# Output projection, feed-forward and down projection with features on partitions, the second norm applied when PSUM is emptied, and four waits moved

## What is computed

```
h = rms_norm(x, g_mix);  z = h @ w_in             # q, k, v (3 groups), u, two gates
a_out = dilated_attention(q, k, v) @ w_attn_proj
y = gelu(s5_ssm(u));  s_out = (y @ w_glu_a) * sigmoid(y @ w_glu_b)
mix = sigmoid(gate_a) * a_out + sigmoid(gate_s) * s_out
x = x + mix @ w_out                               # "x1" in the kernel
h2 = rms_norm(x, g_ffn)
x = x + (silu(h2 @ w_ffn_gate) * (h2 @ w_ffn_up)) @ w_ffn_down     # D_FF = 2816
```

## Time and profile before

| | |
|---|---|
| median of three runs | 916.68 us |
| the profiled execution | 918.38 us, its span 916.5 us |
| PE busy | 885.2 us, 97% of the span |
| DVE, ACT, POOL busy | 423.3, 349.1, 178.6 us |
| mean share of the 16 DMA engines busy | under 40% |
| mean granted clock of TensorE | 0.993 |

### The profile page before, as it was taken

How to read it: one execution, slowest core, us unless ns; L and a number is a source line. 1 busy time by engine, 2 the same in 40 slices (tenths; PEclk the granted TensorE clock), 3 DMA queues, 4 the chain that set the end, 5 groups by cost and what they waited for, 6 DMA issues and landing times.

```text
span 916.5 us, 12956 instructions
## 1 busy us (share of the span) xinstructions
PE 885.2 (97%) x4488; PEld 726.2 (79%) x4488; DVE 423.3 (46%) x583; ACT 349.1 (38%) x514; POOL 178.6 (19%) x223
## 2 busy tenths in 40 slices
PE   5988999999999999998999989999999999999998
PEld 4876888888797877876887867888888888888886
DVE  6575566677804444543468344322223222333333
ACT  5311343323325656754533235333333333322221
POOL 4699978710020000001220020000000000000000
PEclk9999999999999999998999999999999999999999
DMA  7338344574454552411224323223322233222222
GB/s 274 106 94 209 117 136 137 150 189 137 143 147 145 168 154 77 133 69 51 106 77 160 115 69 92 92 92 98 108 92 92 92 104 102 92 92 92 92 69 92
DMA packets 84511, 106.64 MB, mean 116 GB/s; under 512 B 10464, under 2 KB 51600, under 8 KB 84480
## 3 DMA queue, kind: packets, MB, share of 16 engines
q1 hardware_dynamic: 79904, 96.34, 33.6%
q10 hardware_dynamic: 3168, 6.29, 2.1%
q0 software_dynamic: 1408, 3.61, 1.9%
HBM read 92.29 MB, written 13.93 MB: 116 GB/s over the span
## 4 chain that ended last, share of the span: by engine, by line
PE 49%; DVE 2%; DMA 1%; ACT 1%; issue 1%; POOL 0%; SPq 0%; POOLq 0%; DVEq 0%; ACTq 0%
PE ps L1407 26%; PE ps L1421 13%; PE ps L1148 10%; DMA late<-in_x 1%; DVE late L1130 1%; DVE w_lo L550 1%; ACT hT_hi L583 0%; PE ps L1373 0%; ACT w_hi L544 0%; DVE late L1073 0%; DVE hT_lo L1079 0%; PE ps L1310 0%; POOL row_ss L415 0%; POOL row_r L416 0%; PE ps L1296 0%
## 5 line engine op out<-in xcount | busy, mean ns | idle before, releaser
L550 DVE TENSOR_TENSOR w_lo<-w_raw,w_hi 128x1024 fp32r<-128x1024 f32 x142 | 199.8, 1408 | 382.1 <-ACT w_hi L544 380.4
L544 ACT ACTIVATE w_hi<-w_raw 128x1024 fp32r<-128x1024 f32 x142 | 150.3, 1059 | 415.4 <-PE ps L1148 174.7
L1148 PE MATMUL ps<-w_hi,hT_hi 128*128 128x512 f32 x352 | 139.1, 395 | 17.2 <-DVE w_lo L550 17.2
L1407 PE MATMUL ps<-hT_hi,w_hi 128*128 128x512 f32 x352 | 137.1, 390 | 2.0 <-DVE hT_lo L787 1.6
L1148 PE MATMUL ps<-w_lo,hT_hi 128*128 128x512 f32 x352 | 138.0, 392 | 0.0
L1148 PE MATMUL ps<-w_hi,hT_lo 128*128 128x512 f32 x352 | 138.0, 392 | 0.0
L1407 PE MATMUL ps<-hT_hi,w_lo 128*128 128x512 f32 x352 | 137.0, 389 | 0.0
L1407 PE MATMUL ps<-hT_lo,w_hi 128*128 128x512 f32 x352 | 136.9, 389 | 0.0
L400 POOL TENSOR_TENSOR early<-early 128x16 f32<-128x16 f32 (+8 forms) x141 | 124.2, 881 | 23.1 <-ACT early L567 12.1
L1148 PEld LDWEIGHTS ps<-w_hi,hT_hi 128*128 128x128 f32 x352 | 66.8, 190 | 33.0 <-DVE w_lo L550 15.0
L1407 PEld LDWEIGHTS ps<-hT_hi,w_hi 128*128 128x128 f32 x352 | 66.1, 188 | 16.4 <-issue 1.8
(11 more groups left out here) (193 smaller groups left out, 1050.5 us busy)
## 6 DMA issues: line engine op xcount, KB each, us to landing
w_raw<-in_w_in SPq DMA_DIRECT2D x112, 256.0 KB, 3.1
w_raw<-in_w_ffn_gate SPq DMA_DIRECT2D x44, 256.0 KB, 2.8
w_raw<-in_w_ffn_up SPq DMA_DIRECT2D x44, 256.0 KB, 3.0
w_raw<-in_w_ffn_down SPq DMA_DIRECT2D x44, 256.0 KB, 2.7
z_d<-early ACTq DMA_DIRECT2D x6, 1024.0 KB, 4.8
late<-z_d SPq DMA_DIRECT2D x96, 64.0 KB
w_raw<-in_w_out SPq DMA_DIRECT2D x16, 256.0 KB, 3.0
z_d<-early SPq DMA_DIRECT2D x3, 1024.0 KB, 6.6
```

The costliest lines, as they stand in the source:

```text
L544: nc.scalar.activation(w_hi[:, j % WSPL], w_raw[:, j % WRAW], ACT.Copy).then_inc(w_hi_done, 1)
L550: nc.vector.tensor_tensor(w_lo[:, j % WSPL], w_raw[:, j % WRAW], w_hi[:, j % WSPL].bitcast(F32), ALU.subtract).then_inc(w_lo_done, 1)
L1148: ins = T.matmul(ps[:, bank0 + m], lhsT, rhs, start=first and h == 0 and k == 0, stop=last and h == 1 and k == 2)
L1407: ins = T.matmul(ps[:, m], (w_hi, w_lo)[b][:, j % WSPL, at_w:at_w + P], h_acts[a][:, 2 * j + h, :], start=j == 0 and h == 0 and k == 0, st ...
```

## The change

- `W_OUT`, and `W_DOWN`, become by feature. `x1` is held with features on partitions (loaded from the transposed copy `xt`), and the output leaves transposed, in eight stores of 256 KB; the host turns it.
- The second norm no longer scales rows ahead of the transposes. `second_row(k)` on ACT rounds x1 times the gain into `h2_hi` and squares x1; `second_lo(k)` on DVE forms `h2_lo`; POOL adds the eight squared tiles; PE sums them over partitions (8 instructions), POOL takes the root, and PE spreads it over partitions (8 instructions) into `norm_all`, between the tiles of the first round of `W_FFN`. DVE multiplies by `norm_all` as it empties each bank (`swiglu`), so it now empties four banks a round and then multiplies by silu, which ACT takes from SBUF.
- The transposes, `normalised`, `turn_lo`, `gained` and the row sums are gone. `W_FFN` reads the new tiles `h2_hi`, `h2_lo`, which lie where `yT` and `aT` were; `W_DOWN` reads `hT_hi`, `hT_lo`. Three small tiles of 16 bytes are removed, so that all behind them moves 96 bytes down: `h2_hi` begins 70,880 bytes behind `hT_hi`, 96 past a multiple of 128.
- `x1_in` is waited for behind `lo(W_OUT + 4)`.
- Moved waits: section 6 is stored ahead of the loads of `W_V1`, and the first tile of `W_QK` is loaded ahead of the wait for `u_d`; two waits for `z_stored` on SP go. DVE runs `lo(W_V1 + 1)` between the second and the third part of `uT`. `back_im` comes one tile earlier. `W_MIX` waits for DVE's emptying of the gate banks, and no longer for the sigmoid.

```diff
+            sp.wait_ge(act_evac, AE_U + 2)
+            sp.wait_ge(dve_evac, 2)
+            store_z(sp, 6, 0)
             for j in range(4):
                 load(W_V1 + j, j, in_cols(7))
             sp.wait_ge(dve_evac, DE_U + 2)
             sp.dma_start(u_d.rearrange("(m p) j c -> p m (j c)", p=P), uT).then_inc(u_stored, 16)
+            load(W_QK, 0, in_cols(0))
             sp.wait_ge(u_stored, 16)
...
-            sp.wait_ge(act_evac, AE_U + 2)
-            store_z(sp, 6, 0)
-            sp.wait_ge(z_stored, 16)
-            for j in range(4):
+            for j in range(1, 4):
                 load(W_QK + j, j, in_cols(0))
...
-            sp.wait_ge(z_stored, 32)
...
             for m in range(4):
+                if m == 2:
+                    lo(W_V1 + 1, 1)
                 dve.wait_ge(gemm_steps, 4 * (W_U + 3) + m + 1)
...
-            z_chunk(6, also=(back_re, back_im))
+            z_chunk(6, also=(back_re, lambda: None, back_im))
...
-            run(columns(w, 2, by_feature, y_acts, by_act(AE_G - 4)))
+            run(columns(w, 2, by_feature, y_acts, by_dve(DE_G - 4)))
...
+            total = x1_sq[:, 0]
+            for k in range(1, KT):
+                pool.wait_ge(x1_squared, k + 1)
+                pool.tensor_tensor(total, total, x1_sq[:, k], ALU.add).then_inc(x1_added, 1)
+                pool.wait_ge(x1_added, k)
+            pool.wait_ge(norm2_eps, 1)
+            pool.tensor_tensor(norm_row[:, :], norm_row[:, :], minus_half[:, 0:1].to_broadcast([P, TB]), ALU.pow
+                               ).then_inc(norm2_done, 1)
...
+            def second_row(k):
+                act.wait_ge(dve_evac, DE_MIX + k + 1)
+                nc.scalar.activation(h2_hi[:, k], x1[:, k], ACT.Copy, scale=gffnT[:, k:k + 1]).then_inc(h2_hi_done, 1)
+                nc.scalar.activation(x1_sq[:, k], x1[:, k], ACT.Square).then_inc(x1_squared, 1)
...
+            for k in range(4, 6):
+                second_row(k)
+            hi(W_FFN + 1, 1)
+            for k in range(6, 8):
+                second_row(k)
...
+            lo(W_FFN + 2, 2)
+            dve.wait_ge(x1_sums, 1)
+            V.tensor_scalar(norm_row[:, :], ps[:, 4, 0:2 * TB].rearrange("p (n e) -> p n e", e=2)[:, :, 0], 1.0 / DM, EPS,
+                            ALU.mult, ALU.add).then_inc(norm2_eps, 1)
+            lo(W_FFN + 3, 3)
+            dve.wait_ge(norm2_spread, 1)
+            V.tensor_copy(norm_all[:, :], ps[:, 5]).then_inc(norm2_eps, 1)
+            lo(W_FFN + 4, 4)
...
             def swiglu(f):
+                for m in range(4):
+                    dve.wait_ge(gemm_steps, 4 * (W_FFN + 3) + m + 1 + 16 * f)
+                    out = sg[:, m] if m < 2 else s_raw[:, bass.ds(f * 2 + m - 2, 1)].rearrange("p b c -> p (b c)")
+                    V.tensor_tensor(out, ps[:, m], norm_all[:, :], ALU.mult).then_inc(ffn_evac, 1)
+                for m in range(2):
+                    dve.wait_ge(silu_done, 2 * f + m + 1)
+                    dve.wait_ge(ffn_evac, 4 * f + m + 3)
+                    s_at = s_raw[:, bass.ds(f * 2 + m, 1)].rearrange("p b c -> p (b c)")
+                    V.tensor_tensor(s_at, s_at, sg[:, m], ALU.mult).then_inc(s_raw_done, 1)
...
+            ffn(0, 0)
+            ffn(0, 1)
+            pe.wait_ge(x1_added, KT - 1)
             pe.wait_ge(dve_evac, DE_OUT)
-            rows_turned(xn2)
+            for n in range(TB):
+                ins = T.matmul(ps[:, 4, 2 * n:2 * n + 2], x1_sq[:, 0, n * P:(n + 1) * P], ones[:, 0:2], start=True, stop=True)
+            ins.then_inc(x1_sums, 1)
+            ffn(0, 2)
+            pe.wait_ge(norm2_done, 1)
...
+            ffn(0, 3)
...
                     for k, (a, b) in enumerate(((0, 0), (1, 0), (0, 1))):
-                        ins = T.matmul(ps[:, m], y_acts[a][:, j % 2, n * P:(n + 1) * P],
-                                       (w_hi, w_lo)[b][:, j % WSPL, h * 512:(h + 1) * 512], start=first and k == 0, stop=last and k == 2,
-                                       skip_group_check=not (first or last))
+                        ins = T.matmul(ps[:, m], (w_hi, w_lo)[b][:, j % WSPL, m * P:(m + 1) * P], h_acts[a][:, j % 2, :],
+                                       start=first and k == 0, stop=last and k == 2, skip_group_check=not (first or last))
```

More of the change, by code:

```diff
@@ L578, in _ @@
                     squares(j // 2)
-            def gained(g):
-                for k in range(KT):
-                    act.wait_ge(x_turned, k + 1)
-                    nc.scalar.activation(hT_hi[:, k], ps[:, k], ACT.Copy, scale=g[:, k:k + 1]).then_inc(hT_hi_done, 1)
             hi(W_V0 + 2, 2)
@@ L839, in _ @@
                                 norm_all[:, :].rearrange("p (c j) -> p j c", j=CL), ALU.mult).then_inc(dve_evac, 1)
-            for j in range(1, 5):
+            for j in range(2, 5):
                 lo(W_V1 + j, j)
@@ L876, in z_chunk @@
                 lo(W_QK + 4 * c + 3, 3)
+                for step in also[2:3]:
+                    step()
                 if not first:
@@ new lines, in residual @@
+            def residual(c):
+                for m in range(4):
+                    dve.wait_ge(gemm_steps, 4 * (W_OUT + 4 * c + 3) + m + 1)
+                    V.tensor_tensor(x1[:, 4 * c + m], x1[:, 4 * c + m], ps[:, 4 * c + m], ALU.add).then_inc(dve_evac, 1)
+            for j in range(1, 5):
+                lo(W_OUT + j, j)
+            dve.wait_ge(x1_in, 16)
+            residual(0)
+            lo(W_OUT + 5, 5)
+            for k in range(4):
+                second_lo(k)
+            for j in range(6, 9):
+                lo(W_OUT + j, j)
@@ L1388, in _ @@
             for c in range(2):
-                run(columns(W_OUT + 4 * c, 4, by_token, h_acts, by_dve(DE_GLU + 4 + 4 * c), split_rows(mix_lo_done, 0)))
-            pe.wait_ge(dve_evac, DE_OUT)
-            rows_turned(xn2)
-            with pe.Fori(0, FB) as f:
-                for j in range(4):
-                    w = W_FFN + j + 4 * f
-                    pe.wait_ge(w_lo_done, w + 1)
-                    for m in range(4):
-                        if j == 0:
-                            if m < 2:
-                                pe.wait_ge(act_evac, AE_GLU - 1 + m + 2 * f)
-                            else:
-                                pe.wait_ge(s_raw_done, 2 * f + m - 1)
-                        turned_rows(KT, j, m)
-                        for h in range(2):
-                            for k, (a, b) in enumerate(((0, 0), (1, 0), (0, 1))):
-                                at_w = m // 2 * 512 + h * 256 + m % 2 * P
-                                ins = T.matmul(ps[:, m], (w_hi, w_lo)[b][:, j % WSPL, at_w:at_w + P],
-                                               h_acts[a][:, 2 * j + h, :], start=j == 0 and h == 0 and k == 0,
-                                               stop=j == 3 and h == 1 and k == 2)
-                        ins.then_inc(gemm_steps, 1)
@@ new lines, in _, with ffn @@
+                run(columns(W_OUT + 4 * c, 4, by_feature, h_acts, by_dve(DE_GLU + 4) if c == 0 else lambda m: None,
+                            split_rows(mix_lo_done, 0), 4 * c))
+            def ffn(f, j):
+                w = W_FFN + j + 4 * f
+                pe.wait_ge(w_lo_done, w + 1)
+                for m in range(4):
+                    if j == 0:
+                        if isinstance(f, int):
+                            pe.wait_ge(dve_evac, DE_MIX + m + 1)
+                        else:
+                            pe.wait_ge(ffn_evac, 4 * f - 3 + m)
+                    if isinstance(f, int) and m == 0:
+                        pe.wait_ge(h2_lo_done, 2 * j + 2)
+                    for h in range(2):
+                        for k, (a, b) in enumerate(((0, 0), (1, 0), (0, 1))):
+                            at_w = m // 2 * 512 + h * 256 + m % 2 * P
+                            ins = T.matmul(ps[:, m], (w_hi, w_lo)[b][:, j % WSPL, at_w:at_w + P],
+                                           (h2_hi, h2_lo)[a][:, 2 * j + h, :], start=j == 0 and h == 0 and k == 0,
+                                           stop=j == 3 and h == 1 and k == 2)
+                    ins.then_inc(gemm_steps, 1)
@@ new lines, in _ @@
+            ffn(0, 0)
+            ffn(0, 1)
+            pe.wait_ge(x1_added, KT - 1)
+            pe.wait_ge(dve_evac, DE_OUT)
+            for n in range(TB):
[3 more added lines that the diff above has]
+            pe.wait_ge(norm2_done, 1)
+            for n in range(TB):
+                ins = T.matmul(ps[:, 5, n * P:(n + 1) * P], norm_row[:, n:n + 1].to_broadcast([P, P]), ident[:, :],
+                               start=True, stop=True)
@@ L1465 @@
     inputs = {name: np.asarray(a) for name, a in inputs.items()}
-    large = {name: a for name, a in inputs.items() if name == "x" or name.startswith("w_")}
+    large = {name: a for name, a in inputs.items() if name.startswith("w_")}
     for name, a in {**large, **parameters(inputs), **constants()}.items():
```

160 lines of the change are left out of this document (61 added, 99 removed).

## The result

| | before | after |
|---|---|---|
| median (lowest to highest) | 916.38 us (915.11 to 917.49) | 902.57 us (901.73 to 906.17) |
| profiled execution, its span | 918.38, 916.5 us | 902.23, 900.4 us |
| PE busy; mean granted clock | 885.2 us (97%); 0.993 | 882.5 us (98%); 1.00 |

The ratio is 0.9857, with a 95% interval of 0.9827 to 0.9887: 13.8 us, or 1.4%, faster (the median of before is now of four runs; the 916.68 was of three). Forecast were 891.7, and at most 899.5. The direction was right and the size was not: the time is 10.9 us above the forecast, and 11.2 us of the forecast gain of 25.0 are missing.

A forecast was written before the change was run, and what follows sets the result against it. PE was 97% busy, so only its gaps and its dense stream's rate could shorten the time. The terms 7.2 + 3.4 + 4.8 + 8.2 - 0.1 + 1.2 + 0.3 = 25.0 us took 916.7 to 891.7; range 888.0 to 899.5.

The forecast's parts named there:

- The rate of the feed-forward: Feed-forward: h2 as moving operand, off the 128-byte grid, costs 0.0022 us more per matmul, 2.3 us lost over 1056.
- a grid of 128 bytes: Dense matmuls: quickest, 0.2267 us, with activations a multiple of 128 bytes from the weights; off it 0.0022 moving, 0.0067 stationary.
- Rival 3: Feed-forward, mix and attention projection: h2 costs as much as the stationary case, 0.0067 a matmul; 897.7 us; chance 0.12.
- The early part: Early waits: gaps before 65.35 and 85.07 and a half clock go, 7.9 us, less 0.7 for POOL; net 7.2.
- Rival 2: Early tiles: POOL holds w_lo at the new places and the 3.2 us gap returns; 895.4 us; chance 0.18.
- The y stage: Gap before 250.76 (1.8 us) and the half clock behind it (1.6) go with back_im earlier; net 3.4.
- rival 1: Mix or y stage: the clock halves all the same, 1.6 + 2.9 us come back; 896.2 us; chance 0.14.
- The mix: Start of the mix: no wait for the sigmoid gives 2.1 us, an unhalved clock 2.9 more; net 4.8.
- From the output projection to the feed-forward: Gap before 503.33 (1.6 us), transposes and row-norm wait (7.6) and slow start (0.1) go; small norm instructions add 1.8.
- Rival 6: Feed-forward: DVE's fuller rounds stop PE once a round by 2 us, 22 in all; 914 to 916 us; chance 0.03.
- rival 5: Feed-forward: moving operand 32 bytes off any 64 is fetched twice; at 0.26 us a matmul 924.6 us; chance 0.03.
- The anchor: Starting time: the profiled span, 916.5 us, stands for the median, 916.68; the profiled execution's extra 1.9 us lies around its span.

The follow-up runs named there:

- e4: The kernel before with 64 unused bytes ahead of the group of tiles that holds yT and aT; 920.59 us.
- e13: The kernel before with 128 unused bytes ahead of the group of yT and aT; 915.3 us.
- e7: The kernel after with the early moves undone (SP's order and waits, all four uT parts ahead of lo(W_V1 + 1)); 908.24 us.
- e12: The kernel after with the second W_QK tile also loaded ahead of the wait for u_d; 899.85 us.
- e14: e12 with back_im alone in its old place; 901.05 us.
- e8: The kernel after with back_im in its old place and W_MIX waiting for the sigmoid again; 907.52 us.
- e10: The kernel before with 192 unused bytes ahead of the group of yT and aT; 912.65 us.
- e9: e1 with the second W_QK tile also loaded ahead of the wait for u_d; 890.56 us.
- e6: e1 with 64 more unused bytes ahead of hT_hi, so that all operands move together; 896.58 us.
- e3: The kernel after with 64 unused bytes ahead of the group of yT, aT and h2; 903.16 us.
- e1: The kernel after with 32 unused bytes ahead of the group of yT, aT and h2; 891.24 us.

## Why the prediction was wrong, step by step

**The rate of the feed-forward: the failed step, 4.6 us.** The forecast took "the row with the same role, moving" for a distance that no row showed, 0.0022 us a matmul. The kernel paid 0.0067: 1056 x 0.0067 = 7.0 and not 2.3. The direction was right, that moving the tiles by 96 bytes costs something, and so was the gain of 3.5 in the down projection. But the reading behind it, a grid of 128 bytes and a role that sets the price, fell with e4 and e13. The rows had three pairs, (0, 0.2267), (64, 0.2288 moving) and (64, 0.2333 stationary), and "the role decides" was one of two readings; the other, that the third pair is 192 when counted from the stationary operand, fits as well and would have called for no guess about roles. Rival 3 had the right rate, for the feed-forward and for the mix.

**The mix and the attention projection: a term left out, 0.9 us.** `yT` and `aT` moved by the same 96 bytes. The forecast wrote 6.0 for both as part of rival 3 and nothing in the sum, though its own rate of the unseen place, if different from 64's, would have applied there as well. 288 matmuls were 0.9 us in the trace of the changed kernel (288 x 0.0044 = 1.3 by the rates).

**The early part: 7.2 forecast, 5.15 in the trace, 5.7 by e7.** The first gap (3.2) went as described, with `w_lo` between the parts of `uT`. The second did not, because only the first `W_QK` tile was freed, and the sentence "now it is issued right behind `u_d`" was true of that one alone. PE needs the second tile 5.4 us later, too soon for one that still stands behind eight loads. Where 0.7 were set against POOL, it took back 2.8: 1.9 at this tile and 0.9 at later ones. Rival 2 had the mechanism, though not its place: it put POOL's hold before 65, where the move worked. e12 shows the whole of it: 2.7 us less than the kernel after, and 8.0 less than before at the end of the chunks (behind the start-up), where the forecast had 7.9 before it took off its 0.7.

**The y stage: 3.4 forecast, 3.6 in the two profiled executions, 1.2 by the medians of e12 and e14.** Gap and half clock went. What is late next was named wrongly: the keys, at 263. It was the values, at 275 to 279, and only in some executions. The half clock in the profile of before was itself one of several outcomes: six profiles have the late `back_im` and a stop of 1.68 or 1.69 us, and it stands behind two of them (before and e13) and not behind four (e4, e8, e10 and e14).

**The mix: 4.8 forecast, 4.8 measured**, 2.1 for the gap and 2.7 for the clock. The stop that stayed, 1.49 us, did not halve the clock, so rival 1 fell. e8 brought it back, with both parts. The 2.7 is one outcome too: behind the same stop of 3.5 us the clock was at 0.50 for 6.8 us in before, e8 and e10, but for 3.4 in e4 and e13; and by the medians e8's 5.0 less e14's 1.2 leaves 3.8 for the mix.

**From the output projection to the feed-forward: right.** 9.3 forecast for the load of x, the transposes and the row norm, 9.0 measured; the eight small instructions twice cost 1.8, as put. This is the seam:

```profile
528.56 0.39 PE L1167 MATMUL ps<-hT_hi,w_lo 128*128 128x512 f32 x1
528.79 0.40 PE L1408 MATMUL ps<-h_hi,w_hi 128*128 128x512 f32 x1
...
546.47 1.05 PE L1423 MATMUL ps<-ident,norm_row 128*128 128x128 f32 x8
547.28 0.47 PE L1408 MATMUL ps<-h_hi,w_hi 128*128 128x512 f32 x1
```

0.23 us from the last matmul of the one stage to the first of the other, where 7.83 had been, and 0.81 for the spread of the norm.

**DVE's fuller rounds: free, as put.** DVE went from 28.79 to 36.87 us in 100, and PE waited for it nowhere in the feed-forward. Rival 6 fell, and rival 5 with it: the unseen place cost 0.0067, not 0.026.

**The tail: 0.3 forecast, 0.5 measured** (4.2 us from the last matmul's start to the end of the span, 3.6 after).

**The anchor: 1.9 us.** The sum was made on one execution and set against the median of others. In each run the time is about 1.8 us above its own span, so the profiled 918.38 was an execution 2 us slower than the median, and terms read from it can be gone in another. The early part shows how: the profiles of e10 and e13, with the same early program though another place of `uc`, have no gap at 85.07 (one of 0.68 us between two starts stands at 79.40 in e10, one of 0.78 in e13), but half clock for 6.8 us behind the gap at 65, where the profile of before has none. The forecast saw the 1.9 us and then explained them away. Which part of that execution held them isn't shown.

The Trainium skill's page "TensorE: Matmul & The Clock Gate" (section "Wait — 56ns, not 53.3ns?") has one time for a warm matmul of a given number of columns, and no address in it. No run here agrees: 226.7, 228.9 and 233.3 ns stand for the same 512 columns, and some 9 us between e12 and e9 hang on it. (Without the forecast's two rate terms the sum would have been 892.9, not 893.0.)

## What to carry to other kernels

A change that adds or removes a small tile moves all tiles behind it. Work out from the sizes what happens to the distance of each pair of operands, measure the rate of each dense stage by the count of matmuls in a fixed stretch, and pad until the pair stands as the quick one does: here 32 unused bytes were worth 9 of the 26 us between the kernel before and the fastest one. Judge a pad by that count and not by the time alone, since it also moves where DMAs land and so who wins a race elsewhere. And where two engines share a resource or a load stands in a queue, ask how near the race is: a wait that was removed in the one execution that was profiled may be one that others never had.

## What the runs showed of the hardware

- A float32r matmul of 128x128 by 128x512 starts every 0.2267, 0.2289 or 0.2333 us at full clock, by the distance of its operands modulo 256 bytes (the table above; at 128 it is 0.2321 to 0.2333), and not by the addresses themselves (e6). A PE that is 100% busy and at clock 1.00 can lose 3% in this way.
- The clock doesn't halve at every stop of the same length. Behind 1.68 us in the y stage it was 0.50 in the profile of before and 1.00 in that of e8; behind the wait for values it was 1.00 in e12 (2.1 us) and 0.50 in e3 (2.2 us).
- A `w_lo` (DVE) that begins inside one of POOL's large instructions ends 1.08 us after that instruction's end, whatever is left of it: 2.26 us in the kernel after, 0.28 in e1, 0.42 in e12. Alone it takes 1.23.
- SP took 4.05 us (e1) to 5.71 us (e4) to issue the same eight `uc` loads, and 6.23 to 7.04 in e12, e9 and e14, where one more weight tile stands ahead of them. They landed 0.84 us apart in e1 and 1.43 in e4. The eight stores to `y_d` from the same arena lean the same way: a median of 3.7 to 3.9 us to landing in e1, e9 and e10, 4.5 to 5.6 in the others.
